# A two-stack transformer forward pass: where the output projection's first chunks, the rotary angles and the gate bounds are computed

## The reference

```python
def first_block(x, ...):                      # DEPTH = 4
    h = x
    for i in range(DEPTH):
        h = h + 0.5 * swiglu(rms_norm(h, norm_ffn1[i]), ffn1_w_gate_up[i], ffn1_w_down[i])
        hn = rms_norm(h, norm_mix[i])
        # i = 0 and 3: stick-breaking attention; 1: MoBA; 2: MLA. 16 heads, each ends with  from_heads(o) @ w_o
        h = h + mix
        h = h + 0.5 * swiglu(rms_norm(h, norm_ffn2[i]), ffn2_w_gate_up[i], ffn2_w_down[i])
    return rms_norm(h, final_norm)

def swiglu(x, w_gate_up, w_down):
    g, u = jnp.split(x @ w_gate_up, 2, axis=-1)
    return (jax.nn.silu(g) * u) @ w_down      # D_FF = 2816

def rotary(x, pos):                           # MoBA (layer 1) and MLA (layer 2); a like one in stack 2
    inv = ROPE_THETA ** (-jnp.arange(0, r, 2) / r)
    ang = pos[:, None] * inv[None, :]
    cos, sin = jnp.cos(ang), jnp.sin(ang)
    ...

# second stack (2 layers): per-token FFNs modulated by  silu(c) @ mod_w + mod_b,  a mixer of differential
# attention (uses exp of the lambda terms), RWKV-7 and HGRN2, whose lower bounds are
lb = jnp.cumsum(jax.nn.softmax(hgrn_lower_bounds, axis=0), axis=0)
lb = lb - lb[0]
```

## Time and profile before

| | us |
|---|---|
| median of 3 runs | 4213.1 |
| lowest and highest | 4210.68, 4216.2 |
| profiled execution | 4215.57 |
| its span, first to last instruction | 4213.8 |
| PE busy in the span | 3863.3 (92%) |
| PE weight loads | 3047.7 (72%) |
| DVE busy | 2216.5 (53%) |
| ACT busy | 1537.0 (36%) |
| POOL busy | 1083.4 (26%) |
| mean granted TensorE clock | 0.945 of full |

### The profile page before, as it was taken

One profiled execution on the slowest core, in us unless ns is written; L12 is line 12 of the kernel. 1 busy time (PEld: TensorE's weight loads), 2 busy tenths in 40 slices (PEclk: granted clock), 3 DMA queues, 4 the chain that ended last, 5 costly groups with the idle time before them and its releaser, 6 DMA issues.

```text
span 4213.8 us, 46679 instructions
## 1 busy us (share of the span) xinstructions
PE 3863.3 (92%) x17647; PEld 3047.7 (72%) x17647; DVE 2216.5 (53%) x2275; ACT 1537.0 (36%) x1895; POOL 1083.4 (26%) x574
## 2 busy tenths in 40 slices
PE   6998999999999899999898997987899997996899
PEld 5865888757887768886587866676787775685777
DVE  6533756426664356653466443536545443537554
ACT  3354443234342434435443321223333321223333
POOL 6500748205564037460082000110000000120000
PEclk9999999999999999999999998988999998987999
DMA  7633767446674257673474542202454542201454
GB/s 246 204 103 117 250 209 249 140 120 225 224 236 160 86 184 251 201 229 90 150 249 140 180 125 82 80 11 90 165 184 160 175 133 79 100 11 55 155 181 138
DMA packets 493252, 649.62 MB, mean 154 GB/s; under 512 B 16075, under 2 KB 393442, under 8 KB 493090
## 3 DMA queue, kind: packets, MB, share of 16 engines
q1 hardware_dynamic: 472356, 569.62, 41.9%
q0 software_dynamic: 19584, 75.50, 5.1%
q10 hardware_dynamic: 1150, 2.29, 0.2%
HBM read 646.29 MB, written 1.05 MB: 154 GB/s over the span
## 4 chain that ended last, share of the span: by engine, by line
issue 61%; POOLq 18%; PE 13%; POOL 6%; SPq 1%; ACT 1%; DVE 0%; DMA 0%; DVEq 0%; ACTq 0%
POOLq L571 7%; POOLq L573 5%; POOLq L575 5%; PE bank L1194 4%; PE bank L895 3%; POOL mod_zone L578 2%; POOL modrow L578 1%; PE bank L1316 1%; PE bank L1330 1%; PE bank L1332 1%; POOL modrow L560 1%; POOL mod_zone L560 1%; PE bank L867 1%; PE bank L874 0%; PE bank L876 0%
## 5 line engine op out<-in xcount | busy, mean ns | idle before, releaser
L1998 DVE TENSOR_TENSOR wproj_lo<-wproj,wproj_hi 128x2048 fp32r<-128x2048 f32 x252 | 748.3, 3006 | 132.0 <-ACT wproj_hi L1538 132.0
L895 PE MATMUL bank<-wproj_hi,x_hi 128*128 128x512 f32 x2112 | 542.3, 399 | 40.7 <-DVE arena L2089 31.0
L895 PE MATMUL bank<-wproj_lo,x_hi 128*128 128x512 f32 x2112 | 534.5, 396 | 0.0
L895 PE MATMUL bank<-wproj_hi,x_lo 128*128 128x512 f32 x2112 | 525.3, 391 | 0.0
L895 PEld LDWEIGHTS bank<-wproj_hi,x_hi 128*128 128x128 f32 x2112 | 398.5, 191 | 137.2 <-issue 48.4
L1578 ACT CAST actT_hi<-bank 128x512 fp32r<-128x512 f32 x132 | 77.4, 587 | 1121.4 <-PE bank L922 1121.4
L535 POOL TENSOR_SCALAR rstd<-sumsq 128x1 f32<-128x1 f32 x38 | 7.5, 197 | 1845.2 <-ACT tok L1521 1845.0
L1538 ACT CAST wproj_hi<-wproj 128x2048 fp32r<-128x2048 f32 x252 | 469.9, 1911 | 13.6 <-DMA wproj<-in_ffn_w_gate_up 13.6
L895 PEld LDWEIGHTS bank<-wproj_hi,x_lo 128*128 128x128 f32 x2112 | 400.0, 189 | 84.4
L895 PEld LDWEIGHTS bank<-wproj_lo,x_hi 128*128 128x128 f32 x2112 | 387.6, 188 | 76.7
L867 PE MATMUL bank<-wproj,xT 128*128 128x384 f32 (+2 forms) x1216 | 425.0, 506 | 7.0 <-issue 4.7
(11 more groups left out here) (417 smaller groups left out, 5360.6 us busy)
## 6 DMA issues: line engine op xcount, KB each, us to landing
wproj<-in_ffn_w_gate_up SPq DMA_DIRECT2D x336, 512.0 KB, 6.1
wdown<-in_ffn_w_down SPq DMA_DIRECT2D x132, 1024.0 KB, 5.0
wproj<-in_w_in SPq DMA_DIRECT2D x52, 1024.0 KB, 6.4
wproj<-in_ffn_w_gate SPq DMA_DIRECT2D x84, 512.0 KB, 5.0
wproj<-in_ffn_w_up SPq DMA_DIRECT2D x84, 512.0 KB, 6.2
mod_zone<-in_mod_w POOLq DMA_DIRECT2D x36, 1024.0 KB, 6.7
modrow<-in_mod_w POOLq DMA_DIRECT2D x36, 1024.0 KB, 7.4
wproj<-in_sb_w_qkv SPq DMA_DIRECT2D x48, 512.0 KB, 5.4
```

The source lines that it names most:

```text
L895: last = nc.tensor.matmul(proj_ps[t][:, :], rounded(x_part[of_x](c)[:, toks]), rounded(w_part[of_w][:, c, :]), start=start and c == 0, sto ...
L1998: V.tensor_tensor(rounded(wproj_lo[w.odd][:, cols]), src[:, cols], wproj_hi[w.odd][:, cols], ALU.subtract).then_inc(cols_lo, 1)
```

## The change

In the last pair of the three first-stack kinds of attention, PE multiplies chunks 0 to 5 of the first weight block for tile 0 before `weigh_values` and for tile 1 after it; `out_proj` then adds chunks 6 and 7 and does the second block as before. The differential attention of the second stack is left as it is. DVE's hooks of the first stack's FFNs move from the end of the step to a place behind `rest_of_rows`, ahead of the wait for `actT_hi`. `take_vectors` goes to step 1 of the first FFN, `terms` is split into steps 2 and 9; the angles go in pieces to steps 0, 1, 2 and 9 of layer 0's second FFN, and `bounds` to its step 10. ACT's `constants` and `angles` go to steps 1 and 10 of that second FFN, its `bounds` to step 1 of layer 1's first FFN. DVE waits for the results before layer 1's attention.

```diff
@@ tensor: attend
+                def out_chunks(t, chunks):
+                    w = Step(n.load + pairs)
+                    if t == 0:
+                        pe.wait_ge(w_in[w.odd], DMA * (n.landed[w.odd] + (2 if kind == "mla" else 3) * pairs // 2 + 2))
+                    rhs = wproj[w.odd][:, :].rearrange("p (c n) -> p c n", c=KC)
+                    for c in chunks:
+                        nc.tensor.matmul(proj_ps[t][:, :], o_all[:, c, t * P:(t + 1) * P], rhs[:, c, :],
+                                         start=(c == 0), stop=False)
...
+                    elif kind == "diff":
+                        weigh_values(i)
                     else:
+                        pe.wait_ge(at_ev, i.n(2, 2))
+                        pe.wait_ge(ot_copied, i.n(1, -1))
+                        out_chunks(0, range(KC - 2))
                         weigh_values(i)
+                        out_chunks(1, range(KC - 2))
@@ tensor: out_proj
-                linear(o_all, kc, WO_BLOCKS, lambda: turn_x(0, False))
+                w = Step(n.load)
+                rhs = wproj[w.odd][:, :].rearrange("p (c n) -> p c n", c=KC)
+                for t in range(NT):
+                    for c in range(KC - 2, KC):
+                        last = nc.tensor.matmul(proj_ps[t][:, :], o_all[:, c, t * P:(t + 1) * P], rhs[:, c, :],
+                                                start=False, stop=(c == KC - 1))
+                    last.then_inc(proj_done, 1)
+                n.loaded(1, 2)
+                n.lin += 1
+                linear(o_all, kc, WO_BLOCKS[1:], lambda: turn_x(0, False))
@@ scalar
-                ffn(False, l == 0, False,
-                    besides={0: conditioning, 2: angles, 9: constants, 10: bounds} if l == 0 else {})
+                ffn(False, l == 0, False, besides=({0: conditioning}, {1: bounds}, {}, {})[l])
...
-                ffn(False, True, True)
+                ffn(False, True, True, besides={1: constants, 10: angles} if l == 0 else {})
@@ vector: ffn
                     rest_of_rows(st)
+                    if k in behind:
+                        behind[k]()
                     v.wait_ge(ff_copied, st.n(1, 1))
...
-                    if k in besides:
-                        besides[k]()
@@ vector: take_vectors and the former constants, now positions, turns, remainders, angles
                 v.wait_ge(vec_turned, 2)
+                v.wait_ge(masks_ready, 1)
...
-            def constants():
-                v.wait_ge(const_in, CONST_DMAS * DMA)
-                v.wait_ge(masks_ready, 1)
+            def positions():
                 V.tensor_copy(pos[:, 1, :], pos_i[:, :])
                 ...
+            def turns():
...
+            def remainders():
...
+            def angles():
...
             def terms():
+                v.wait_ge(const_in, CONST_DMAS * DMA)
...
+            def term_sums():
@@ vector: the first stack's loop
-                    besides={0: take_vectors, 1: constants, 2: terms, 10: bounds} if l == 0 else {})
+                    behind={1: take_vectors, 2: terms, 9: term_sums} if l == 0 else {})
                 enter_mix(1, gained(3 * l + 1), False)
-                if l == 0:
+                if l == 1:
                     v.wait_ge(low_s, 2)
...
-                    ffn(True, lambda: enter_ffn(0, gained(3 * l + 3), False))
+                    ffn(True, lambda: enter_ffn(0, gained(3 * l + 3), False),
+                        behind={0: positions, 1: turns, 2: remainders, 9: angles, 10: bounds} if l == 0 else {})
```

More of the change, by code:

```diff
@@ L2074, in copy_even, with ffn @@
                 n.odd += (kc + 1) // 2 // 2
-            def ffn(ffn_next, then, row=None, rows={}, layer=None, besides={}):
+            def ffn(ffn_next, then, row=None, rows={}, layer=None, behind={}):
                 scaled = row is not None
@@ L2685, in take_vectors @@
                 v.sem_inc(vec_ready, 1)
-            def constants():
-                v.wait_ge(const_in, CONST_DMAS * DMA)
-                v.wait_ge(masks_ready, 1)
+            split = NROPE - DH // 2
+            def positions():
                 V.tensor_copy(pos[:, 1, :], pos_i[:, :])
@@ L2693, in constants @@
                 v.drain()
-                split = NROPE - DH // 2
                 for stack, (a, b) in enumerate(((0, split), (split, NROPE))):
```

## The result

The changed kernel takes **4164.9 us** (median of 4 runs, 4160.6 to 4168.9) beside 4214.7 for the kernel before on the same chip (4 runs, 4210.7 to 4218.9): ratio 0.9875, 95% interval 0.9858 to 0.9893, 49.7 us less. The forecast was 4159, range 4150 to 4176. The profiled execution took 4168.86 us, the slowest of the four, against 4215.57: 46.7 less. First the page's busy shares of the changed kernel, beside the earlier trace rows.

A forecast was written before the change was run, and what follows sets the result against it. TensorE, busy 92% of the span, was taken as the bound, so only its idle or slow-clock time counts. Gains of 28.5 (projection) and 25.3 us (angles) sum to 53.8 off 4213.1: 4159 us, range 4150 to 4176.

The forecast's parts named there:

- signs against it: New L874 wait for L2095, first-FFN L895 wait for a DMA, or layer 0's second FFN over 5 us longer.
- Projection, MoBA and MLA: Last attention pair to FFN2: 32.1 us instead of 38.5 (MoBA) and 39.0 (MLA), gains 6.4 and 6.9 us.
- Projection, stick-breaking: Last pair to FFN2 in two layers: gain 7.6 us each, between 9.1 and 6.0.
- lower case: Stick-breaking last pair: clock falls, values and early chunks lose 1.0 + 2.1 us, gain 6.0 us.
- Part 1: Output projection around the last pair, four layers: gain 28.5 us, ends 24 and 33.
- First FFN: Layer 0's first FFN without the angles: 25.5 us gained, plus 0.8 from moving `take_vectors`.
- Second FFN: Layer 0's second FFN takes over the angles: costs 1 us, ends 0 and 5.
- rival 1: Last softmax, all four layers: clock falls, 6 us lost each, only the FFN part pays; 4183 us, chance 8%.
- Rival 2: First FFN meets shorter waits for its weights: 14 us go, gain 40, 4173 us, chance 6%.
- Rival 3: Pieces ahead of L2095 hold back `actT_lo`, from fifteen blocked whole by POOL: slower, 4221 us, chance 2%.
- Rival 4: Clock stays high in all last pairs, second FFN pays nothing: gain 60 us, 4153 us, chance 10%.
- part 2: Angles and small operations moved in layer 0's two FFNs: gain 25.3 us, ends 20 and 27.

The follow-up runs named there:

- e1: The kernel before with only the early output-projection chunks in the last attention pair: 4179.9 us against 4216.9, ratio 0.9914.
- e5: The kernel before with POOL's first modulation tiles in the first FFN held back until step 4: 4231.2 us, ratio 1.0033.
- e2: The kernel before with only the scalar and vector operations moved and cut up, output projection as before: 4198.3 us, ratio 0.9954.
- e3: The changed kernel with tile 1's six early chunks put back behind the last output transposes: 4176.8 us, ratio 0.9904.
- e4: The changed kernel with DVE's moved pieces at the end of each step, ahead of the SwiGLU products: 4183.4 us, ratio 0.9918.
- e6: The changed kernel with two tile 1 chunks between the two heads' probability transposes, stick-breaking layers only: 4157.2 us, ratio 0.9864.
- e8: The changed kernel with the edits of e6 and e7 together: 4137.1 us, ratio 0.9809.
- e7: The changed kernel with the second half of each column block's rest behind the next step's SwiGLU products, all FFNs: 4143.5 us, ratio 0.9827.

## Why the prediction was right, and which terms were off

The sum was 53.8 us, measured 49.7; both parts pay, in the places named, and none of the signs against it appeared. PE's waits for the products fell to 11.6 us, forecast about 9. The terms measured in their stages make 29.3 + 23.0 − 0.1 = 52.2 us; other stages, which the forecast didn't name, take 5.5 of them back in the traces (46.7), most of it in the second stack. That the medians come out at 49.7, so near the sum, is in part luck. By its steps:

- **Projection, MoBA and MLA:** 32.1 us worked out, 31.2 measured twice. The values took 1.4 instead of 1.6 us, the wait for ACT's copy 0.24 instead of 0.38, and the twenty calls with `turn_x` 17.7 instead of 18.0; the gain is 7.3 and 7.7 instead of 6.4 and 6.9.
- **Projection, stick-breaking:** 7.6 each, the middle between "clock holds" (9.1) and "clock falls" (6.0). It fell in both layers. In layer 0 it cost 3.0 us, as the lower case had it (3.1), and 6.8 were gained only because the other pieces were 0.8 us cheaper than priced. In layer 3 the transposes and the values ran at full speed and the second six took 7.07 us, 1.7 us too long; 7.6 were gained. So the middle was met by two errors against each other. Part 1 as a whole: 29.3 by the stages, forecast 28.5.
- **First FFN:** this is the mis-sized term, 26.3 forecast and 23.0 measured. I took the earlier trace rows as showing that an idle of 3.20 us leaves the clock alone, and "waits under 1 us" as the next thing late. From step 2's first matmul to the sums it is 201.87 − 47.02 = 154.9 us instead of 150.7. The two groups behind 2.49 us of idle are 1.12 and 0.63 us longer than the 1.98 of full speed, the two behind 1.87 us 0.97 and 0.79, and that wait is 0.9 us above the 1.0 us of waits in the second FFN: 4.4 by these rows, 4.1 measured. Ahead of step 2 the place of `take_vectors` was to give 0.8, and 1.6 came (48.62 − 47.02). But e1 and e5, which leave it where it was, start step 2 at 47.43 and 47.54, so most of the 1.6 isn't its work. Five profiles have the angles out of this FFN (changed, e2, e3, e4, e6), and they gain 22.1 to 26.1 us by its end; the forecast's 26.3 lies just outside.
- **Second FFN:** forecast 1 us, measured 0.1. The Trainium skill's page SBUF — State Buffer, section "Who interferes with whom", was right on the stretching: three operations of 0.22 us took 3.44, 2.46 and 1.35, and each ended less than 0.1 us after the POOL operation beside it (412.73, 415.26 and 416.69). Its "whoever starts first" shows in the row block's rest, which starts with POOL's L570 in both kernels: before, POOL took 3.60 us and DVE 5.75; in the changed kernel DVE, 0.01 us ahead, took 2.29 and POOL 5.75. It doesn't show in the operation of 4.55 us, which I took for it: that started at 74.69, POOL's L570 only at 75.49, and still DVE ended last, 0.14 us after POOL. The stretching made the price of the operations, not of the stage: DVE idled there otherwise (3.89 us in the earlier trace rows), and the row block's rest gave it another 3.46, so the 7.25 us of `turns` just fitted. e4 shows the 13.5 us that the pieces cost in another place.

The row block's rest beside POOL's L570, in the kernel before and then in the changed one:

```profile
436.75 5.75 DVE L2003 TENSOR_TENSOR wdown_lo<-wdown,wdown_hi 128x2048 fp32r<-128x2048 f32 x1
436.75 3.60 POOL L570 TENSOR_TENSOR modrow<-modrow,cond 128x2048 f32<-128x2048 f32 x1 [20.15 <-DVE arena L2089]
```

```profile
406.97 2.29 DVE L2027 TENSOR_TENSOR wdown_lo<-wdown,wdown_hi 128x2048 fp32r<-128x2048 f32 x1
406.98 5.75 POOL L570 TENSOR_TENSOR modrow<-modrow,cond 128x2048 f32<-128x2048 f32 x1 [20.18 <-DVE arena L2113]
```

- **ACT:** its constants at 420.2 to 423.4 delayed the Silu to 424.67 and nothing behind it, as forecast.
- **Rivals:** rival 1 (clock low in all four) was true in the two stick-breaking layers, for 3.0 and 1.7 us and not 6 each. Rival 2 (weights) did not show: no L895 wait for a load in the first FFN. Rival 3 needs fifteen operations blocked whole; in the second FFN the three of `turns` were stretched to 3.44 us at most, the three of `remainders` took 2.41 us together instead of 0.97 (e5), and the others 0.6 us at most. Rival 4 had the second FFN right (0.1 us) and the clock in the stick-breaking layers wrong.

What the first FFN's term meant was less sure than I wrote: e1 got 11.7 of the same microseconds with nothing changed there. The kernel before has them in its one profile by how DVE and POOL met there. Had it met as in e1, part 2 would show less. That the long meeting is the more usual one is hinted at, not shown: e2's median, 18.6 us under that of eleven runs of the kernel before, doesn't hang on that profile, and part 1's 29.7 us off 4216.9 make 4187.2, which lies in e1's slower group. How often each meeting happens in runs without a profile stays open.

## What to carry to other kernels

Work that is ready should stand between the short waits of a latency chain, not only in the longest: in MoBA the second six chunks had 0.77 us of idle to fill and gained 2.7 us, 1.6 of them by the clock (from the second six on, the projection's 44 records up to `turn_x` took 20.7 us in e3 and 19.0 in the changed kernel). Small operations on an engine that shares its way with another belong in the idle stretch behind the last thing that the bottleneck waits for, not ahead of it; the same pieces cost 0.1 us in one place and 13.5 in the other. Before an engine is delayed to be out of the way, look for its own deadline.

## What the runs showed of the hardware

- The length of a burst of small DVE operations beside POOL differed with how the two engines met: the same instructions took 16.8 us (before), 7.6 (e1) and 4.2 (e5, POOL idle). The blocking goes both ways: between the same two operations POOL sat 3.86 us in e1 while DVE ran through, and 1.26 us in the kernel before.
- Idles of 0.24, 0.77 and 0.46 us among sparse small matmuls were followed by a granted clock of 0.72 in e3; 0.94 us behind six dense chunks was not (three transposes at 0.55). In the first FFN 3.20 us left the speed alone in the kernel before (2.12 us for eight records), while 2.49 us did not in the changed one (3.10). Nor does one length of idle settle it: behind 1.86 or 1.87 us at the same place in step 5 the eight records took 2.10 (e4), 2.51 (e2), 2.95 (changed), 3.35 (e3) and 3.62 us (e6).
- From POOL's last tile to the sums that it releases it was 6.0 us in e5 (227.57 to 233.60), 6.1 in e8 (199.16 to 205.24) and 6.6 in e7 (199.47 to 206.06), with one DMA issue of 0.92 us between: what a stage waits for on POOL has to be done that much earlier.
- With DVE's large operations split around the products (e7), POOL's nine tiles in the first FFN came 16.6 to 17.3 us apart (the first L570 at 49.36, the last at 184.77) instead of 13.9 to 17.2 in the changed kernel (47.50, 171.66), though DVE's work was the same. What makes the difference isn't shown.
